# A hybrid attention layer on one core: query-key products in three passes of split operands, factors of later heads moved, last values copied behind the rounding

## The reference

```python
s = jnp.einsum('bhqcd,bhkcd->bhcqk', qb, k).astype(jnp.float32) * scale   # differential
p = jax.nn.softmax(s, axis=-1)
a = p[:, :, 0] - lam * p[:, :, 1]
...
s = jnp.einsum('bhqd,bhqkd->bhqk', qb, kg).astype(jnp.float32) * scale     # dilated
...
a_o = rms_norm(a_o, a_out_norm)
b_o = rms_norm(b_o, b_out_norm) * (1.0 - lambda_init)
```

## Time and profile before

| what | value |
| --- | --- |
| median of 3 runs | 1806.03 us (1805.72 to 1807.71) |
| the profiled execution | 1805.4 us |
| its span, first to last instruction | 1803.7 us |
| PE busy | 1797.5 us (100%) |
| DVE, ACT busy | 1551.3 us (86%), 1071.2 us (59%) |
| granted TensorE clock, mean | 1.000 |
| attention between units of the projection | 777 to 1056 us of the span |

### The profile page before, as it was taken

The page is one execution under the profiler, slowest core; times in us unless marked ns, Lnnn a source line. Parts: engine busy times, 40 slices in busy tenths (PEclk is TensorE's granted clock), DMA queues, the critical chain, the costliest instruction groups (busy, mean ns, idle before and its releaser), DMA issues.

```text
span 1803.7 us, 22784 instructions
## 1 busy us (share of the span) xinstructions
PE 1797.5 (100%) x8227; PEld 1491.4 (83%) x8227; DVE 1551.3 (86%) x1614; ACT 1071.2 (59%) x1295; POOL 43.6 (2%) x73
## 2 busy tenths in 40 slices
PE   9999999999999999999999999999999999999999
PEld 7888888888888888888888888888888888888887
DVE  6899999999999888657666666799999999998986
ACT  6565665666665564556566655566666666666553
POOL 0000000000000000111010000000000000000000
PEclk9999999999999999999999999999999999999999
DMA  9665565554446566654555445755566656354654
GB/s 358 209 215 210 198 217 190 188 207 163 140 164 246 196 211 211 199 178 164 164 164 187 141 164 186 257 192 204 188 215 216 217 189 218 106 187 163 237 206 141
DMA packets 178406, 351.95 MB, mean 195 GB/s; under 512 B 7184, under 2 KB 8224, under 8 KB 178080
## 3 DMA queue, kind: packets, MB, share of 16 engines
q1 hardware_dynamic: 178304, 351.02, 55.9%
q10 hardware_dynamic: 32, 0.01, 0.0%
HBM read 348.91 MB, written 2.10 MB: 195 GB/s over the span
## 4 chain that ended last, share of the span: by engine, by line
PE 99%; DVE 0%; ACT 0%; issue 0%; POOL 0%; DVEq 0%; POOLq 0%
PE acc L537 14%; PE acc L539 14%; PE acc L538 14%; PE acc L599 8%; PE acc L598 8%; PE acc L597 8%; PE turn L611 4%; PE turn L612 4%; PE turn L610 4%; PE acc L612 3%; PE acc L611 3%; PE acc L610 3%; PE turn L568 1%; PE turn L695 1%; PE turn L694 1%; PE turn L696 1%
## 5 line engine op out<-in xcount | busy, mean ns | idle before, releaser
L1307 DVE TENSOR_TENSOR w_lo<-w_raw,w_hi 128x1024 fp32r<-128x1024 f32 x167 | 205.0, 1238 | 131.0 <-ACT w_hi L926 130.5
L926 ACT ACTIVATE w_hi<-w_raw 128x1024 fp32r<-128x1024 f32 x166 | 175.4, 1059 | 197.2 <-PE acc L539 178.2
L943 ACT ACTIVATE w_hi<-b 128x1024 fp32r<-128x1024 f32 x200 | 212.6, 1063 | 118.8 <-PE acc L599 77.2
L957 ACT ACTIVATE w_hi<-w_raw 128x1024 fp32r<-128x1024 f32 x176 | 185.5, 1059 | 121.2 <-PE acc L539 88.4
L599 PE MATMUL acc<-w_hi,h_lo 128*128 128x512 f32 x640 | 249.0, 389 | 0.0
L597 PE MATMUL acc<-w_hi,h_hi 128*128 128x512 f32 x640 | 249.0, 389 | 0.0
L598 PE MATMUL acc<-w_lo,h_hi 128*128 128x512 f32 x640 | 249.0, 389 | 0.0
L1328 DVE TENSOR_TENSOR w_lo<-w_raw,w_hi 128x1024 fp32r<-128x1024 f32 x176 | 213.0, 1222 | 31.3 <-ACT w_hi L957 27.6
L1318 DVE TENSOR_TENSOR w_lo<-b,w_hi 128x1024 fp32r<-128x1024 f32 x200 | 236.5, 1219 | 0.0
L943 ACT ACTIVATE w_hi<-w_raw 128x1024 fp32r<-128x1024 f32 x160 | 169.5, 1061 | 91.7 <-PE acc L599 64.1
L1318 DVE TENSOR_TENSOR w_lo<-w_raw,w_hi 128x1024 fp32r<-128x1024 f32 x160 | 193.8, 1222 | 15.4 <-ACT w_hi L943 12.3
(11 more groups left out here) (218 smaller groups left out, 3266.1 us busy)
## 6 DMA issues: line engine op xcount, KB each, us to landing
w_raw<-in_ffn_w_in SPq DMA_DIRECT2D x94, 1024.0 KB, 5.1
w_raw<-in_ffn_w_out SPq DMA_DIRECT2D x88, 1024.0 KB, 5.1
b<-in_ffn_w_in SPq DMA_DIRECT2D x80, 1024.0 KB, 5.1
w_raw<-in_w_in SPq DMA_DIRECT2D x48, 1024.0 KB, 5.1
w_raw<-in_w_out SPq DMA_DIRECT2D x16, 1024.0 KB, 4.9
w_raw<-in_ffn_w_in SPq DMA_DIRECT2D x4, 512.0 KB, 6.9
x_sb<-in_x SPq DMA_DIRECT2D x3, 512.0 KB, 9.0
out_y<-x_sb SPq DMA_DIRECT2D x3, 512.0 KB, 8.3
```

What stands on the lines that cost most here:

```text
L926: nc.scalar.activation(w_hi[:, u % RING, 0:count, :], w_raw[:, slot, k0:k0 + count, :], ACT.Copy).then_inc(hi_ready, 1)
L943: nc.scalar.activation(w_hi[:, slot, :, :], in_raw(piece)[:, k0:k0 + UK, :], ACT.Copy).then_inc(hi_ready, 1)
L957: nc.scalar.activation(w_hi[:, u % RING, :, :], src, ACT.Copy).then_inc(hi_ready, 1)
L1307: nc.vector.tensor_tensor(w_lo[:, slot, 0:count, :], w_raw[:, v // 2 % RAW, k0:k0 + count, :], w_hi[:, slot, 0:count, :].bitcast(F32), ALU ...
```

## The change

Queries and keys get a high part (ACT, `round_qk`, in place of the copy) and a low part (DVE, `split_qk`, new, two operations behind ACT's). The product of each half of the queries is three F32R passes, and the two 64-row products of a differential head alternate. Both `values` and `scores` now wait for DVE's `qk_split`. The norm of finished heads is divided in factors and scaling, and for groups 0 and 1 the scaling comes one phase later, for group 2 both do. `scale_qk` moves from behind the two units of its part to ahead of them, and there it also stands ahead of `turn_mixed`. The last `copy_chunk` moves into the tail, behind ACT's rounding of head 12.

```diff
@@ -224,7 +224,7 @@
             mask = sb("mask", [P, TT, SEQ], F32, attention)
             probs = sb("probs", [P, 2, TT, SEQ], F32, attention)
             weights = sb("weights", [P, TT, SEQ], F32, attention)
-            qk_t = sb("qk_t", [P, 2, SEQ], F32, attention)
+            qk_hi = sb("qk_hi", [P, 2, SEQ], F32R, attention)
             w_t = sb("w_t", [P, TT, SEQ], F32, attention)
             head_sq = sb("head_sq", [P, TT, HD], F32, attention)
             head_ss = sb("head_ss", [P, TT * HEADS_C], F32, attention)
@@ -242,6 +242,7 @@
             neg_lam_inv = sb("neg_lam_inv", [P, 2], F32, attention)
             norm_col = sb("norm_col", [P, KD], F32, attention)
             norm_in = sb("norm_in", [KD, P], F32, attention)
+            qk_lo = sb("qk_lo", [P, 2, SEQ], F32R, attention)
 
 
         acc = [ctx.enter_context(nc.psum_tensor(f"acc{i}", [P, TT, NC], F32)) for i in range(2)]
@@ -321,7 +322,8 @@
         qk_normed = sem("qk_normed")
         col_ready = sem("col_ready")
         qk_turned = sem("qk_turned")
-        qk_t_ready = sem("qk_t_ready")
+        qk_hi_ready = sem("qk_hi_ready")
+        qk_split = sem("qk_split")
         scored = sem("scored")
         max_ready = sem("max_ready")
         probs_ready = sem("probs_ready")
@@ -800,16 +802,17 @@
                 mm.then_inc(qk_turned, 1)
 
             def scores(u):
-                pe.wait_ge(qk_t_ready, u + 1)
+                pe.wait_ge(qk_split, u + 1)
                 if u:
                     pe.wait_ge(probs_ready, u)
                 subs = 2 if u < B_HEADS else 1
                 width = HD // subs
-                for c in range(subs):
-                    part = slice(c * width, (c + 1) * width)
-                    for t in range(TT):
-                        mm = nc.tensor.matmul(score[:, c, t, :], qk_t[part, 0, t * P:(t + 1) * P],
-                                              qk_t[part, 1, :], start=True, stop=True)
+                for t in range(TT):
+                    for n, (q, k) in enumerate(((qk_hi, qk_hi), (qk_hi, qk_lo), (qk_lo, qk_hi))):
+                        for c in range(subs):
+                            part = slice(c * width, (c + 1) * width)
+                            mm = nc.tensor.matmul(score[:, c, t, :], q[part, 0, t * P:(t + 1) * P], k[part, 1, :],
+                                                  start=n == 0, stop=n == 2)
                 mm.then_inc(scored, 1)
 
             def turn_weights(u):
@@ -826,7 +829,7 @@
                 pe.wait_ge(w_t_ready, u + 1)
                 wait_read(pe, QKV, 3 * g + 2)
                 if u + 1 < HEADS:
-                    pe.wait_ge(qk_t_ready, u + 2)
+                    pe.wait_ge(qk_split, u + 2)
                 for t in range(TT):
                     for kt in range(TT):
                         mm = nc.tensor.matmul(head_acc[:, t, :], w_t[:, kt, t * P:(t + 1) * P],
@@ -1157,7 +1160,7 @@
                     wait_read(act, QKV, q)
                     nc.scalar.activation(squares[:, :, :], qkv[:, g % 2, kind, :, :], ACT.Square).then_inc(qk_squared, 1)
 
-            def copy_qk_t(u):
+            def round_qk(u):
                 act.wait_ge(qk_turned, u + 1)
                 if u:
                     act.wait_ge(scored, u)
@@ -1165,8 +1168,8 @@
                     act.wait_ge(col_ready, 3)
                 for a in range(2):
                     n = a + (TT if u < B_HEADS else 0)
-                    s = nc.scalar.activation(qk_t[:, a, :], qk_turn[:, a, :], ACT.Copy, scale=gain_col[:, n:n + 1])
-                s.then_inc(qk_t_ready, 1)
+                    s = nc.scalar.activation(qk_hi[:, a, :], qk_turn[:, a, :], ACT.Copy, scale=gain_col[:, n:n + 1])
+                s.then_inc(qk_hi_ready, 1)
 
             def exps(u):
                 act.wait_ge(max_ready, u + 1)
@@ -1214,7 +1217,7 @@
                 u, phase = divmod(s, 3)
                 if phase == 0:
                     if u < HEADS:
-                        copy_qk_t(u)
+                        round_qk(u)
                     if 1 <= u <= HEADS:
                         copy_w_t(u - 1)
                 if phase == 1:
@@ -1271,9 +1274,10 @@
 
                         act.wait_ge(lam_sums, 1)
                         nc.scalar.activation(lam[:, 2:4], lam[:, 0:2], ACT.Exp).then_inc(lam_exps, 1)
-            copy_chunk(3 * GROUPS - 1)
             for s, n, count in tail():
                 attention_step(s - 1)
+                if s == SEG * (GROUPS - 1) + 1:
+                    copy_chunk(3 * GROUPS - 1)
                 split_hi(PROJ, n + 4, n + count + 4, PARTS_D)
             attention_step(SEG * GROUPS + 2)
             for v in range(sum(TAIL) + 4, 2 * len(PROJ_ORDER) + 4):
@@ -1731,6 +1735,17 @@
                                                 .to_broadcast([P, heads, width]), ALU.mult)
                 s.then_inc(qk_scaled, 1)
 
+            def split_qk(u):
+
+                dve.wait_ge(qk_hi_ready, u + 1)
+                if u == 0:
+                    dve.wait_ge(col_ready, 3)
+                for a in range(2):
+                    n = a + (TT if u < B_HEADS else 0)
+                    s = nc.vector.scalar_tensor_tensor(qk_lo[:, a, :], qk_turn[:, a, :], gain_col[:, n:n + 1],
+                                                       qk_hi[:, a, :].bitcast(F32), ALU.mult, ALU.subtract)
+                s.then_inc(qk_split, 1)
+
             def maxima(u):
 
                 dve.wait_ge(scored, u + 1)
@@ -1768,10 +1783,13 @@
                                                        masked[:, t, :], ALU.mult, ALU.add)
                 s.then_inc(weights_ready, 1)
 
-            def norm_heads(g, first=0, last=HEADS_C):
+            def head_factors(g, first=0, last=HEADS_C):
 
                 dve.wait_ge(head_copied, HEADS_C * g + last)
                 inverse_root(head_rstd[:, TT * first:TT * last], head_ss[:, TT * first:TT * last], HD)
+
+            def scale_heads(g, first=0, last=HEADS_C):
+
                 for n in range(first, last):
                     for t in range(TT):
                         o = rows[:, g % 2, t, n * HD:(n + 1) * HD]
@@ -1784,6 +1802,8 @@
             def attention_step(s):
 
                 u, phase = divmod(s, 3)
+                if phase == 0 and u < HEADS:
+                    split_qk(u)
                 if phase == 1 and u < HEADS:
                     maxima(u)
 
@@ -1794,11 +1814,18 @@
                     if u < HEADS:
                         finish_weights(u)
                     if u == HEADS - 1:
-                        norm_heads(GROUPS - 1, 0, HEADS_C - 1)
+                        head_factors(GROUPS - 1, 0, HEADS_C - 1)
+                        scale_heads(GROUPS - 1, 0, HEADS_C - 1)
                     if u == HEADS:
-                        norm_heads(GROUPS - 1, HEADS_C - 1)
-                if phase == 2 and 0 < u < HEADS and u % HEADS_C == 0:
-                    norm_heads(u // HEADS_C - 1)
+                        head_factors(GROUPS - 1, HEADS_C - 1)
+                        scale_heads(GROUPS - 1, HEADS_C - 1)
+                g = u // HEADS_C - 1
+                if phase == 2 and 0 <= g < GROUPS - 2 and u % HEADS_C == 0:
+                    head_factors(g)
+                if phase == 0 and 0 <= g < GROUPS - 1 and u % HEADS_C == 1:
+                    if g == GROUPS - 2:
+                        head_factors(g)
+                    scale_heads(g)
 
             def turn_mixed(s):
 
@@ -1830,6 +1857,8 @@
                     s = SEG * (g - 1) + j - 1
                     if s >= 0:
                         attention_step(s)
+                    if j in (6, 9):
+                        scale_qk(2 * g + j // 9)
                     if turned_at(s):
                         turn_mixed(s)
                     v = 2 * (SEG * g + j) + 4
@@ -1840,8 +1869,6 @@
                     if g == 0 and j == 1:
                         turn_split_lo(ROWS[R_NORMX] + 3, h_hi, h_lo, 12, xg_at[3])
                         norm_factor(1)
-                    if j in (6, 9):
-                        scale_qk(2 * g + j // 9)
                     if g == 0 and j == 10:
                         negative_lambda()
             for s, n, count in tail():
```

## The result

The changed kernel takes 1815.03 us (median of 5 runs, 1813.79 to 1815.37) and the kernel before 1807.02 (5 runs beside it, 1805.72 to 1807.71): a ratio of 1.0046, with a 95% interval of 1.0035 to 1.0057. That is 8.0 us slower. 4.5 were forecast, and the time lies 2 us above the range.

A forecast was written before the change was run, and what follows sets the result against it. PE was taken to bound the kernel, so its waits add in full. Gains of 3.15 us less losses of 7.6 gave net 4.5 us slower, forecast as 1810.2 us, with an 8 in 10 range of 1806.8 to 1813.

The forecast's parts named there:

- Direction: Whole kernel: slower than before, net 4.5 us, with a chance of 0.71.
- the waits at heads 6 and 10: PE's weight turns wait for `mix_lo`, now behind `scale_qk` on DVE: losses of 3.45 and 2.43 us.
- the clock falls in the new gap: Rival, 7%: PE's gaps at heads 6 and 10 bring 1.2 GHz, losing 1.5 to 3 us: 1812 to 1813.
- The tail: Norm of heads 8 to 11 ends later, so `mix_lo` delays PE's turn of head 13's weights: 0.75 us lost.
- The forecast's own figure for the end of the norm: On DVE in the tail, the norm of heads 8 to 11 was to end at 1022.90 instead of 1019.56.
- its own last sentence: Signs of error: `mix_lo` wait under 1 us, score passes 0.2 us apart, or a wait not counted.
- The pass: Scores on PE: a 256-column F32R pass was counted at 0.1135 us.
- heads 8 to 15: Scores of these eight heads in split F32R passes: a gain of 1.5 us.
- heads 0 to 7: Scores as six pairs of passes, 0.40 + 6 x 0.1135 = 1.08 us a head: 1.5 us gained in eight.
- The pairs side by side: Scores of heads 0 to 7: 64-row F32R passes pair; the rival that they don't (8%) gave 1815.7 us.
- the 0.15 of the copy: Last values: moving the copy of chunk 11 behind ACT's rounding of head 12 gives back 0.15 us.
- The small waits at `qk_lo`: PE's values of heads 1, 2 and 6 wait for `qk_lo` behind `scale_qk` and two units: 1.0 us together.

The follow-up runs named there:

- The first experiment: The changed kernel with `turn_mixed` (`mix_lo`) ahead of `scale_qk` again; 1806.42 us, ratio 1.0002 to the kernel before.
- e6: The changed kernel with two unread 128 x 512 additions on DVE ahead of `mix_lo` in group 3, lengthening PE's wait at head 10; 1817.36 us.
- e3: The changed kernel with `turn_mixed` ahead of `scale_qk` again and the norms of finished heads in one piece at their old place; 1809.97 us.
- e4: The kernel before with the split passes only: `scale_qk`, the norms and the last chunk copy at their old places; 1824.28 us.
- e5: The changed kernel with `mix_lo` between the two last operations of `scale_qk` in group 2, shortening PE's wait at head 6; 1815.19 us.
- e2: The changed kernel with `scale_qk` back at its old place behind both units of its part; 1819.48 us.

## Why the prediction was wrong

**Direction, and the waits at heads 6 and 10: right.** `mix_lo` was forecast to end at 896.83 and ended at 896.80; PE stood 3.34 us, as forecast. At head 10 the standing is 2.31 (976.79 + 0.23 to 979.33), forecast 2.32. The first experiment shows that these two waits and what hangs on them are 8.0 of the 8.4 us.

**The clock: the step that failed.** The forecast gave "the clock falls in the new gap" 7%, and priced it at 1.5 to 3 us. The sum held nothing for it. The price held (2.68), in part by luck: it took a stretch at the low clock as long as the gap, and the stretch was 6.8 us, twice as long. The chance was too low. Its ground was the earlier trace rows: PE idle for 3.3 us at the end of the program, granted clock 1.00. That view ended with the last instruction. The clock record goes on, and shows the fall 0.7 us later (at 1804.34, 4.0 us behind PE's last matmul). In the trace of before:

```profile
1800.40:1803.60 3.20, 0.00 (x0) 0.00 (x0) 0.69 (x2) 0.00 (x0) 0.00 (x0) 1.00 0.42 164
1804.40:1805.60 1.20, 0.00 (x0) 0.00 (x0) 0.00 (x0) 0.00 (x0) 0.00 (x0) 0.50 0.00 0
```

and in that of after, where PE stands as long at the end (3.38 us in both), it is already inside the span, 2.1 us behind PE's last matmul:

```profile
1808.90:1810.70 1.80, 0.00 (x0) 0.00 (x0) 0.58 (x1) 0.00 (x0) 0.00 (x0) 1.00 0.55 215
1810.90:1812.00 1.10, 0.00 (x0) 0.00 (x0) 0.00 (x0) 0.00 (x0) 0.00 (x0) 0.50 0.13 48
```

A fall that comes with the end of a gap costs nothing at the end of a program and a stretch of half-speed passes in the middle. The row that I read as evidence against the rival was silent on it: at the ends of the twelve traces, all with 3.4 us from PE's last matmul to the end of the span, the fall comes anything from 2.1 to 4.2 us behind that matmul. The Trainium skill (TensorE: Matmul & The Clock Gate, Why this matters for your kernels) advises against idle gaps of some microseconds between bursts of matmuls. The four waits of 3.4 us and more agree with it, and behind six of the sixteen shorter ones (2.1 to 2.9 us) the clock fell too (below).

**The tail: right in kind, wrong in place and size.** The forecast followed the norm to the maxima and the turned weights of head 13, and got 0.75 (0.70 when laid bare). It didn't follow ACT, which waits for `rows_ready` ahead of `copy_head(12)`. Before the change the norm had ended at 1019.56, and the copy stood 0.25 behind it, directly behind a rounding:

```profile
1018.85 1.06 ACT L926 ACTIVATE w_hi<-w_raw 128x1024 fp32r<-128x1024 f32 x1 [1.34 <-PE acc L539]
1019.81 0.61 ACT L1203 ACTIVATE rows<-turn,row_inv 128x128 f32<-128x128 f32 x2
```

So it was on time by little. The forecast's own figure for the end of the norm, 1022.90, was good to 0.4 us: it ended at 1030.25, with PE 7.7 us later by then (waits and clock of 9.8 less gains of 2.1). The forecast should have asked who else waits for the norm. The term measured 1.57 and not 0.75, and this wait for the sums of squares is one that the forecast had not counted, which by its own last sentence was a sign of being wrong.

**The pass: the upper bound.** An F32R pass of 256 columns takes 0.119 (six in 0.71), the bound from 0.227 less one F32 stream, and not half of 0.227. With 0.119 the forecast for heads 8 to 15 would be 1.25 (measured 1.20), and for heads 0 to 7 1.27 less 0.40 + 6 x 0.119, 1.2 in all (1.38). The pairs side by side, the 0.40 around them, and the 0.15 of the copy held.

**The small waits at `qk_lo`: 1.2 for 1.0,** at the three heads named. Head 2 was measured at 0.62 (0.5), heads 1 and 6 at 0.34 and 0.24 (0.25 each).

**The whole.** With the clock's 2.7 us left out, the time would be 1812.3, inside the range. The range reached to 1813, and so held the clock's fall (1810.2 + 2.7 = 1812.9) only where every other term came out as forecast. The span is 3.9 us over the forecast's 4.5. The other 0.9 of the 4.8 us by which the time is off comes from adding to one execution: the median of the five runs lies 1.2 us above the profiled one. The forecast allowed 0.6 for that in its words and 0.3 in its sum (1809.9 and 0.6 make 1810.5, and not 1810.2).

## What to carry to other kernels

When a job is moved up on a queue, list all that it passes, and price each by what waits for it; here one move was needed against six waits of 2.2 us and cost 6 us at two others because it passed one operation too many. When an operation ends later, look for everyone who waits for it, on all engines: a wait with 0.25 us to spare in the old trace is the next one. And a wait of TensorE over 2 us can have a second price, the passes at half clock behind it (10 of 20 such waits here had it); read the clock past the end of the span before taking a gap at the end as evidence.

## What the runs showed of the hardware

**The clock behind a wait isn't a matter of its length alone.** All waits of PE over 2 us in the region of the attention, in the six traces that have them, and the stretch at PEclk 0.50 behind each:

| wait | where | fell | stretch |
|---|---|---|---|
| 3.42 to 3.98 us | head 6 (after, e6), head 10 (e6), values of head 12 (e3) | 4 of 4 | 3.4 us twice, 6.8 us twice |
| 2.91 and 2.94 | values of head 12 (e4), head 6 (e5) | 1 of 2 (e5) | 3.4 |
| 2.14 to 2.38 | head 10 (after, e5), six each in e2 and e4 | 5 of 14 | 3.4 each |

A stretch of 3.4 us cost 1.2 to 1.6 us, one of 6.8 us 2.6 to 2.7. The clock fell 2.1 to 4.3 us behind the last matmul before the wait, in six of the ten cases only after PE had started again (up to 1.6 us after). In the two cases of 6.8 us it fell 0.8 and 1.0 us before PE started again; in the eight of 3.4 us it fell at most 0.5 us before, or later. Waits of the same length at the same place fell in one execution and not in another (head 10, 2.37 and 2.38). What decides it these runs don't show.

**The 64-row passes don't need to be neighbours to pair.** With six passes of one half ahead of six of the other, TensorE began the other half's three places early: nine places of 0.117 us, where strict turns would be twelve and perfect pairs six. Going in and out of the 64-row form costs about 0.4 us a head in either order.
